# Two transformer blocks in float32 halves: row steps and row starts of the matmul operands changed

## What is computed

```python
def hybrid_layer(x, ...):                       # first block
    proj = rms_norm(x, norm1_w) @ w_in          # 2048 -> 5648
    ... attention (8 heads of 128), Mamba-2 scan (16 heads of 64)
    x = x + concatenate([attn, ssm]) @ w_out    # 2048 -> 2048
    u = causal_dwconv(rms_norm(x, norm2_w) @ w_up, ...)   # 2048 -> 2 * 5632
    u_gate, u_val = split(u, 2)
    return x + (silu(u_gate) * u_val) @ w_down  # 5632 -> 2048

def second_block(x, meta_tokens, ...):          # 16 meta tokens ahead: 272 positions
    h = concatenate([meta, x])
    z = rmsnorm(h, g_pre_mix) @ w_in            # 2048 -> 6592
    mix = concatenate([short_conv(z), rwkv7(z)]) @ w_out
    h = h + rmsnorm(mix, g_post_mix)
    gate, up = split(rmsnorm(h, g_pre_ffn) @ w_gate_up, 2)
    f = (silu(causal_dwconv_2(gate, conv_ffn)) * up) @ w_down
    return (h + rmsnorm(f, g_post_ffn))[:, 16:]
```

## Time and profile before

| | us |
|---|---|
| median of 3 runs | 2490.83 (2490.74 to 2492.6) |
| the profiled execution | 2490.57 |
| its span, first to last instruction | 2488.8 |
| PE busy | 2470.6 |
| weight loads busy | 2379.1 |
| DVE busy | 1662.9 |
| ACT busy | 1205.5 |

### The profile page before, as it was taken

The page is one execution under the profiler, slowest core; times in us unless marked ns, Lnnn a source line. Parts: engine busy times, 40 slices in busy tenths (PEclk is TensorE's granted clock), DMA queues, the critical chain, the costliest instruction groups (busy, mean ns, idle before and its releaser), DMA issues.

```text
span 2488.8 us, 61026 instructions
## 1 busy us (share of the span) xinstructions
PE 2470.6 (99%) x25716; PEld 2379.1 (96%) x25716; DVE 1662.9 (67%) x2174; ACT 1205.5 (48%) x1450; POOL 59.5 (2%) x69
## 2 busy tenths in 40 slices
PE   9999999999999999999999999999999999999999
PEld 9989999999999999999999999999999999999997
DVE  7776667677777777788856655667656666556666
ACT  6646545555555555455523333346444444444444
POOL 0000000000000000004100000001000000000000
PEclk9999999999999999999999999999999999999999
DMA  7545556666666665666533333354655555655553
GB/s 229 163 145 156 150 166 191 198 193 193 192 193 191 189 197 187 190 193 176 160 107 103 104 96 105 111 170 153 208 181 185 182 181 176 190 181 185 179 182 129
DMA packets 397851, 420.57 MB, mean 169 GB/s; under 512 B 15422, under 2 KB 372530, under 8 KB 397554
## 3 DMA queue, kind: packets, MB, share of 16 engines
q1 hardware_dynamic: 397170, 416.46, 54.3%
q10 hardware_dynamic: 528, 1.84, 0.2%
HBM read 416.15 MB, written 2.10 MB: 168 GB/s over the span
## 4 chain that ended last, share of the span: by engine, by line
PE 96%; DVE 2%; ACT 1%; issue 1%; POOL 0%; ACTq 0%; POOLq 0%
PE psum L2572 26%; PE psum L2573 26%; PE psum L2574 26%; PE psum L2588 3%; PE psum L2587 3%; PE psum L2586 3%; PE psum L3050 2%; PE psum L3156 1%; PE psum L3146 1%; PE psum L3275 0%; DVE w_lo L1378 0%; PE psum L3197 0%; PE psum L3281 0%; PE psum L2818 0%; PE psum L2997 0%
## 5 line engine op out<-in xcount | busy, mean ns | idle before, releaser
L2572 PE MATMUL psum<-act_hi,w_hi 128*128 128x256 f32 (+3 forms) x4736 | 1350.1, 285 | 3.7 <-DVE act_lo L1416 2.9
L2573 PE MATMUL psum<-act_lo,w_hi 128*128 128x256 f32 (+3 forms) x4736 | 1333.5, 282 | 0.0
L2574 PE MATMUL psum<-act_hi,w_lo 128*128 128x256 f32 (+3 forms) x4736 | 1332.5, 281 | 0.3 <-issue 0.3
L1378 DVE TENSOR_TENSOR w_lo<-raw,w_hi 128x1024 fp32r<-128x1024 f32 x788 | 961.2, 1230 | 475.6 <-ACT w_hi L750 474.5
L750 ACT ACTIVATE w_hi<-raw 128x1024 fp32r<-128x1024 f32 x788 | 829.2, 1057 | 908.5 <-PE psum L2574 764.0
L2572 PEld LDWEIGHTS psum<-act_hi,w_hi 128*128 128x128 f32 x4736 | 894.1, 189 | 12.0 <-issue 3.5
L2573 PEld LDWEIGHTS psum<-act_lo,w_hi 128*128 128x128 f32 x4736 | 895.9, 189 | 3.6 <-issue 2.2
L2574 PEld LDWEIGHTS psum<-act_hi,w_lo 128*128 128x128 f32 x4736 | 894.3, 189 | 0.0
L2573 PE MATMUL psum<-ff_lo_rows,w_hi 128*128 128x256 f32 x640 | 176.8, 276 | 0.0
L2574 PE MATMUL psum<-ff_hi_rows,w_lo 128*128 128x256 f32 x640 | 176.8, 276 | 0.0
L2572 PE MATMUL psum<-ff_hi_rows,w_hi 128*128 128x256 f32 x640 | 176.8, 276 | 0.0
(11 more groups left out here) (431 smaller groups left out, 1926.9 us busy)
## 6 DMA issues: line engine op xcount, KB each, us to landing
raw<-in_w_in SPq DMA_DIRECT2D x188, 512.0 KB, 3.8
raw<-in_w_up SPq DMA_DIRECT2D x176, 512.0 KB, 4.5
raw<-in_w_down SPq DMA_DIRECT2D x176, 512.0 KB, 3.6
raw<-in_w_gate_up SPq DMA_DIRECT2D x176, 512.0 KB, 3.5
raw<-in_w_out SPq DMA_DIRECT2D x64, 512.0 KB, 3.5
x_rows<-in_x SPq DMA_DIRECT2D x8, 256.0 KB, 6.9
out_x<-out_rows SPq DMA_DIRECT2D x8, 256.0 KB, 2.6
raw<-in_w_in SPq DMA_DIRECT2D x4, 384.0 KB, 3.4
```

The lines of the kernel that those rows point to most:

```text
L1378: dve.tensor_tensor(w_lo[:, slot], raw[:, slot], w_hi[:, slot].bitcast(F32), ALU.subtract).then_inc(S["lo_done"], 1)
L2572: pe.matmul(out_, wh, xh, start=first and r == 0, stop=False)
L2573: pe.matmul(out_, wh, xl, start=False, stop=False)
L2574: mm = pe.matmul(out_, wl, xh, start=False, stop=last and r == RK - 1)
```

## The change

- `w_hi` and `w_lo` get rows of 272 elements, of which 256 are used: a unit's four rows now lie 1088 bytes apart. `raw` stays as it was. The instructions that write the halves take four rows of 256 elements in place of 1024 elements in a run.
- All stages read activations with the row step of 272 elements: `IN1` and `FFN1` share a start of 48, `MIX` gets 48, `IN2` gets 36. `ff_*_rows` and `last_*_rows` become four rows of 272 elements with start 0. `ssm_hi` and `ssm_lo` keep their step of 256.
- The second block's feed-forward reads 258 columns for the second value as well (`xs` in place of `vals`): two columns more in each of those matmuls. Their results stand two columns further in PSUM and `leave` reads them from there (`at=lead`).
- `rows_unit` moves two rows of 256 columns, 1088 bytes apart, in place of 512 in a run.
- To make room, `y_r` shares `head_sq`, and `p1` to `p4` become one tensor `p`, updated in place. The waits are the same.

The places become: `w_hi` 32896, `w_lo` 50304, `act_hi` 85120, `act_lo` 102784, `ff_hi_rows` 156736, `last_hi_rows` 165440; again multiples of 64 bytes. No instruction is added, removed or moved on any engine; only shapes and addresses differ.

```diff
-    w_hi = sb("w_hi", [P, NSLOT, RK * 256], F32R)
-    w_lo = sb("w_lo", [P, NSLOT, RK * 256], F32R)
+    w_hi_rows = sb("w_hi", [P, NSLOT, RK, T2], F32R)
+    w_lo_rows = sb("w_lo", [P, NSLOT, RK, T2], F32R)
+    w_hi, w_lo = w_hi_rows[:, :, :, 0:256], w_lo_rows[:, :, :, 0:256]
...
-    IN1_HI, IN1_LO = act_rows(44, T1)
-    FFN1_HI, FFN1_LO = act_rows(48, T1)
-    IN2_HI, IN2_LO = act_rows(4, T2)
-    MIX_HI, MIX_LO = [t[:, :, 0:T3] for t in act_rows(0, T2)]
+    IN1_HI, IN1_LO = [t[:, :, 0:T1] for t in act_rows(48, T2)]
+    FFN1_HI, FFN1_LO = IN1_HI, IN1_LO
+    IN2_HI, IN2_LO = act_rows(36, T2)
+    MIX_HI, MIX_LO = [t[:, :, 0:T3] for t in act_rows(48, T2)]
...
-            ("ff_hi_rows", [4 * T1 + 64], F32R), ("ff_lo_rows", [4 * T1 + 64], F32R),
-            ("last_hi_rows", [4 * T1 + 64], F32R), ("last_lo_rows", [4 * T1 + 64], F32R),
+            ("ff_hi_rows", [4, T2], F32R), ("ff_lo_rows", [4, T2], F32R),
+            ("last_hi_rows", [4, T2], F32R), ("last_lo_rows", [4, T2], F32R),
...
-    FF_AT = dict(ffn1=0, ffn2=32)
...
-    LAST_HI, LAST_LO = [M[t][:, 2:2 + 4 * T1].rearrange("p (k t) -> p k t", t=T1)
-                        for t in ("last_hi_rows", "last_lo_rows")]
+    FF_HI, FF_LO = M["ff_hi_rows"][:, :, 0:T1], M["ff_lo_rows"][:, :, 0:T1]
+    LAST_HI, LAST_LO = M["last_hi_rows"][:, :, 0:T1], M["last_lo_rows"][:, :, 0:T1]
...
-                act.activation(w_hi[:, slot], raw[:, slot], ACT.Copy).then_inc(S["hi_done"], 1)
+                act.activation(w_hi[:, slot], raw_rows(slot), ACT.Copy).then_inc(S["hi_done"], 1)
...
-                    at = 256 * r + shift * c
-                    wh, wl = w_hi[:, slot, at:at + m], w_lo[:, slot, at:at + m]
+                    at = shift * c
+                    wh, wl = w_hi[:, slot, r, at:at + m], w_lo[:, slot, r, at:at + m]
...
-                    wh = w_hi[:, slot, 512 * r:512 * r + 512]
-                    wl = w_lo[:, slot, 512 * r:512 * r + 512]
+                    wh, wl = w_hi[:, slot, 2 * r:2 * r + 2], w_lo[:, slot, 2 * r:2 * r + 2]
...
-                vals = [t[:, :, T - T1:T] for t in xs]
...
-                        if by_rows and j >= 2:
-                            group(v + 4 * j, g + j, (pair0 + j) % 2, vals, T1)
-                        else:
-                            group(v + 4 * j, g + j, (pair0 + j) % 2, xs, T)
+                        group(v + 4 * j, g + j, (pair0 + j) % 2, xs, T)
...
-                        unit(u + 12 + k, k, 3, *vals, 4 * k, T1, k == 0, k == 3)
+                        unit(u + 12 + k, k, 3, *xs, 4 * k, T, k == 0, k == 3)
```

More of the change, by code:

```diff
@@ L261, in two_blocks @@
         ("cb", [4, P], F32), ("b_rows", [2, P], F32), ("state0", [2, 512], F32),
-        ("y_r", [2, T1], F32), ("head_sq", [2, T1], F32),
+        ("head_sq", [2, T1], F32),
         ("head_r", [4, T1], F32), ("soft", [2, 8], F32),
@@ L914, in ssm_norm @@
                     act.wait_ge(S["yn_inv"], g + 1)
-                    act.activation(M["y_r"][:, g], M["y_r"][:, g], ACT.Sqrt) \
+                    act.activation(M["head_sq"][:, g], M["head_sq"][:, g], ACT.Sqrt) \
                         .then_inc(S["yn_rstd"], 1)
@@ L1020, in while_up @@
                     hi_group(v + 8)
-                    product_hi(i - 1, v, ff_rows(name)[0])
+                    product_hi(i - 1, v, FF_HI)
                     hi(v + 12, 0)
@@ L1383, in lo_group, with bank_pair, leave @@
                     lo(u + j, j)
-            def bank_pair(pair, T, rows_=P):
-                return psum[0:rows_, 2 * pair:2 * pair + 2, 0:T]
-            def leave(u_end, pair, dst, T, rows_=P, how="scaled", single=False, t0=0):
+            def bank_pair(pair, T, rows_=P, at=0):
+                return psum[0:rows_, 2 * pair:2 * pair + 2, at:at + T]
+            def leave(u_end, pair, dst, T, rows_=P, how="scaled", single=False, t0=0, at=0):
                 dve.wait_ge(S["unit_used"], u_end)
-                src = bank_pair(pair, T, rows_)
+                src = bank_pair(pair, T, rows_, at)
                 if single:
@@ L1720, in ssm_norm @@
                     dve.wait_ge(S["yn_ss"], g + 1)
-                    link(dve.tensor_scalar(M["y_r"][:, g], psum[:, 4, 0:T1], 1.0 / 512, EPS,
+                    link(dve.tensor_scalar(M["head_sq"][:, g], psum[:, 4, 0:T1], 1.0 / 512, EPS,
                                            ALU.mult, ALU.add))
-                    dve.reciprocal(M["y_r"][:, g], M["y_r"][:, g]).then_inc(S["yn_inv"], 1)
+                    dve.reciprocal(M["head_sq"][:, g], M["head_sq"][:, g]).then_inc(S["yn_inv"], 1)
                     for e in range(2):
@@ L1729, in ssm_norm @@
                                 out=proj[:, 32 + j], in0=proj[:, 32 + j], scalar=col(c_snorm + j),
-                                in1=M["y_r"][:, g], op0=ALU.mult, op1=ALU.mult) \
+                                in1=M["head_sq"][:, g], op0=ALU.mult, op1=ALU.mult) \
                                 .then_inc(S["yn_done"], 1)
@@ L2360, in stage @@
                     dve.wait_ge(*own_at("ldt", i))
-                    dve.tensor_tensor(M["p1"][0:RB], M["ldt"][0:RB], over(M["ident32"][0:RB], 1, 4),
+                    dve.tensor_tensor(M["p"][0:RB], M["ldt"][0:RB], over(M["ident32"][0:RB], 1, 4),
                                       ALU.add).then_inc(done_at, 1)
@@ L2368, in stage @@
                     dve.tensor_copy(M["l4t"][0:RB], four(4, P)).then_inc(done_at, 1)
-                    dve.tensor_tensor(M["p2"][0:RB], four(4, 2 * P), M["p1"][0:RB], ALU.add) \
+                    dve.tensor_tensor(M["p"][0:RB], four(4, 2 * P), M["p"][0:RB], ALU.add) \
                         .then_inc(done_at, 1)
@@ L2373, in stage @@
                     dve.wait_ge(*own_at("p2", i))
-                    dve.tensor_tensor(M["p3"][0:RB], four(4, P), M["p2"][0:RB], ALU.add) \
+                    dve.tensor_tensor(M["p"][0:RB], four(4, P), M["p"][0:RB], ALU.add) \
                         .then_inc(done_at, 1)
@@ L2378, in stage @@
                     dve.wait_ge(*own_at("p3", i))
-                    dve.tensor_tensor(M["p4"][0:RB], four(4, 0), M["p3"][0:RB], ALU.add) \
+                    dve.tensor_tensor(M["p"][0:RB], four(4, 0), M["p"][0:RB], ALU.add) \
                         .then_inc(done_at, 1)
@@ L3331, in _ @@
                         out_ = psum[:, 2 * ((g0 + 1) % 2) + c, 0:T3]
-                        at = 256 * r + P * c
-                        wh, wl = w_hi[:, 2 + j, at:at + P], w_lo[:, 2 + j, at:at + P]
+                        at = P * c
+                        wh, wl = w_hi[:, 2 + j, r, at:at + P], w_lo[:, 2 + j, r, at:at + P]
                         k = 8 + 4 * j + r
```

31 lines of the change are left out of this document (15 added, 16 removed).

## The result

| | before | after |
|---|---|---|
| median, us | 2491.62 (4 runs) | 2508.25 (4 runs, 2507.3 to 2510.13) |
| profiled execution, us | 2490.57 | 2509.05 |
| its span, us | 2488.8 | 2507.3 |

The ratio is 1.0068, 95% interval 1.005 to 1.0085: the change makes the kernel slower by 0.5 to 0.85%, where 0.6% faster was forecast. The time is outside the range.

The account below looks back on a forecast made before the run. PE, busy 99% at full clock, was taken as the bound, so time is matmul count times start spacing. Gains of 8.8 + 1.3 + 2.0 + 3.2 = 15.3 us from 2490.83 gave 2475.5 us, range 2462 to 2499.

Parts of the forecast that it names:

- First feed-forward and the attention half of `w_out`: 6528 matmuls of 16 pieces before and after, expected to stay at 113.3 ns: no cost, upper bound +5.5 us.
- The rule of pieces: All stages: spacing is (64-byte pieces touched + 1) x 6.67 ns, a little more where the distance between rows changes.
- The input product: First input product, start aligned, 17 pieces become 16: 8.8 us gained, bounds 3.3 and 11.5.
- the last chunk: Last chunk of the first block: 192 matmuls go from 120.0 to 113.3 ns, 1.3 us gained.
- The 258 columns: Second block: still 17 pieces but constant distance, 120.7 to 120.0 ns, 2.0 us gained, bounds 0 and 4.4.
- second value: Second block, 2016 matmuls from 256 to 258 aligned columns: 121.6 to 120.0 ns, 3.2 us gained, or 1.8 at 120.7.
- RWKV: Its 260 and 272 columns keep start and pieces, only the distance becomes constant: nothing, bounds -1.3 and +1.3 us.
- the 512 columns: `w_down` by rows, 1056 matmuls now moving two rows of 256: nothing, bounds +7.0 and -2.5 us.
- ACT and DVE: Writing four rows of 256 may add start-up per instruction; waiting covers it, and shared buffers add no wait.
- Rival D: First feed-forward falls from 113.3 ns to a second spacing of 117.5, +27.4 us; net +18.4, 2509 us; chance 0.17.
- Rival C: Addresses do not decide the spacing; only two columns more in 2016 matmuls remain, +1.7 us, 2492.5 us; chance 0.08.

Follow-up runs that it names:

- breaks_in_ffn1: Kernel before with one to four small matmuls ahead of each group of the first feed-forward's loop, addresses unchanged; 2527.03 us.
- columns_outer: Changed kernel with the loop order within a unit turned, column half outside and row inside; 2510.15 us.
- slot_shift: Kernel before with 64 bytes more between the slots of the weight halves, rows within a slot still 1024 bytes apart; 2518.72 us.
- after_starts_16: Changed kernel with the activations of all stages at start 16 (second input product 4); 2513.21 us.
- two_columns_less: aligned_1024 with the last two of 258 columns left out in 3840 matmuls of the second feed-forward, output incomplete; 2463.68 us.
- act_step_alone: Changed kernel with the weight halves back at 1024 bytes from row to row, activations keeping 1088; 2506.26 us.
- aligned_1024: Kernel before, 1024-byte steps, with input product and last chunk starts aligned and second value as 258 aligned columns; 2480.64 us against 2491.07.
- starts_b: Kernel before, 1024-byte steps, other aligned activation starts: distances 192 in input product, 0 and 192 in feed-forward products, 128 in last chunk; 2526.13 us.

## Why the prediction was wrong

- **The step that failed** is "First feed-forward and the attention half of `w_out`", costed at nothing "since the other five keep their distance", with an upper bound of +5.5. It measured +23.5 us. The bound came from the second block, where a shifting distance costs 0.85 ns over 120.0; but that stream has no fast rate to lose. 113.3 is not what an aligned row costs by its pieces. It is one of the rates that such a stream can be in, and `breaks_in_ffn1` takes it away from half the groups with every address in place. What the runs show is that a step other than 1024 bytes, of the weights or of the activations alone, loses it in this stage with the changed kernel's starts; that the price does not go by the number of changes (`columns_outer`); and that one change in 24 can be enough (`slot_shift`). They do not show why: that any change of distance excludes the fast rate is refuted by the 528 matmuls of `after_starts_16`.
- **The rule of pieces** had a right half and a wrong one. Two columns in a 17th piece cost 3.8 ns (`two_columns_less`), two more in the same piece nothing (`act_step_alone`), and with 16 pieces the input product (119.2 to 116.8) and the last chunk (120.0 to 116.9) were faster, though there the distance changed too. The wrong half is that 16 pieces have one spacing: I fitted the rule to 113.3, the fast rate, and they take anything from 113.3 to 120.0.
- **The input product** was given 8.8 us and brought 4.0. The mixture of 113.3 and 117.8 that I took from the scan's half of `w_out` is what `aligned_1024` shows, in the stage that I used it for; the changed kernel has 116.9 and 118.0 there.
- **The 258 columns**, given 2.0 us, brought nothing, and the **second value**, given 3.2, brought 1.6, its other bound of 1.8. A shift at every row is not what they pay for.
- **RWKV, the 512 columns, ACT and DVE** at nothing: within their bounds (-0.9 and -0.8 us for the first two; the lower bound of the 512 columns, one matmul in three a piece shorter, should have been -2.3). No effect of the shared `p` and `head_sq` shows.
- **Rival D** named the stage and the sign: the first feed-forward loses 113.3. It gave 2509 against 2508.25, but that is partly luck: the stream did not fall into the second rate of 117.5, it took up the uneven 116.9, so that the 6528 matmuls cost 23.5 us against D's 27.4, and D's gain of 5.2 in the second block was 1.6. I gave it 0.17 because I weighed how many loads were changed (one in six) and not whether the rate can survive a single one. The rows that I had, 71 matmuls at 113.2 and 71 at 117.5 from the same tensors with the same step, already said that 113.3 is a state.
- **The Trainium skill's rule** of independent read ports ("TensorE: Matmul & The Clock Gate", section "Step-by-step: what each phase is for"), by which a weight load takes nothing from the running matmul, does not hold for this kernel. Rival C rested on it. With equal columns and steps the spacing goes from 117.8 to 120.0 when only the activations move (`starts_b`), and from 117.7 to 119.6 when only the weights do (`slot_shift`). Of the section "Back-to-back issue gap" the prediction took the formula by columns alone; it stands there for a single matmul, and of a stream of loads and matmuls the section says that both set the spacing. It has no address in either.

What stays open: what in a break chooses the rate, why distances of 64 and 192 have a fast one, and what makes the 116.9 of the changed kernel. Larger steps that are multiples of 256 bytes, which would keep the distance for 272-column rows, were not tried.

## What to carry to other kernels

When a kernel is bound by a stream of matmuls with a weight load each, read the spacing of starts by stage, and ask of the fastest stage whether it runs at a rate that all its like could have, or in a state that a change of addresses, or a small matmul in between, takes away. A change of layout for a slow stage has to be weighed first against the fast stages that share the buffer. Here starts on multiples of 64 bytes, a moving row that does not run two columns into the next 64, and the relation of the two operands' starts were worth 16 us without any change of step.

## What the runs showed of the hardware

- Two rates of one stream: 256 aligned columns with a weight load each at a constant distance of 64 run at 113.3 or 117.8 ns, from break to break, with no address differing (`breaks_in_ffn1`). At 192 the same two were seen, the fast one for 47 matmuls (`starts_b`), and once for 528 at 113.6 with a row step of 1088 bytes (`after_starts_16`).
- The distance between the moving and the stationary rows, modulo 256 bytes, moves the rate of 256 columns (120.0, 113.3 or 117.8, 118.7, 113.3 or 117.8 for 0, 64, 128, 192) and of 512 columns otherwise: 226.9 at 0, 232.9 at 64.
- Two columns beyond a 64-byte boundary cost 3.8 ns, where two columns at 2.4 GHz are 0.8 (`two_columns_less`); 260 columns cost no more than 258 (120.0 and 120.8, `act_step_alone`).
